# Router logits on four column strips and turned back, ranks by pairwise broadcast comparison, sums zeroed by ScalarE: a two-layer encoder trunk on one core

## The reference

```
logits = t @ router_w + router_b                     # 256 x 1024 by 1024 x 16
probs  = softmax(logits).reshape(N, 4, 4)            # 4 groups of 4 experts
group_score = top_k(probs, 2)[0].sum(-1)
g_sel  = argmax(group_score)
in_group = probs of group g_sel                      # 4 values
w_top, i_top = top_k(in_group, 2); w_top /= w_top.sum()
out[token] = sum over its 2 experts of w * (silu(x @ w_gate[e]) * (x @ w_up[e])) @ w_down[e]
```

## Time and profile before

| | us |
|---|---|
| median of 3 runs | 1472.39 |
| lowest, highest | 1471.46, 1472.82 |
| the profiled execution | 1469.38 |
| its span, first to last instruction | 1467.6 |
| PE busy | 1160.6 (79%) |
| DVE busy | 411.4 (28%) |
| ACT busy | 169.8 (12%) |
| POOL busy | 21.4 (1%) |
| mean granted TensorE clock | 0.876 |

### The profile page before, as it was taken

How to read it: one execution, slowest core, us unless ns; L and a number is a source line. 1 busy time by engine, 2 the same in 40 slices (tenths; PEclk the granted TensorE clock), 3 DMA queues, 4 the chain that set the end, 5 groups by cost and what they waited for, 6 DMA issues and landing times.

```text
span 1467.6 us, 30503 instructions
## 1 busy us (share of the span) xinstructions
PE 1160.6 (79%) x13016; PEld 662.9 (45%) x13016; DVE 411.4 (28%) x1293; ACT 169.8 (12%) x411; POOL 21.4 (1%) x58
## 2 busy tenths in 40 slices
PE   2799978767989779766799868788679987788675
PEld 0684434434545335333374754344345654354332
DVE  0597063211222212121611141642112231121115
ACT  0003110000111001000101130111011110010001
POOL 3100000000000000000000000000000000000000
PEclk7899968888999889888889999769889998899887
DMA  9809859999999999999954301759999699999980
GB/s 373 352 19 422 358 234 408 426 424 426 366 395 413 426 426 423 423 427 421 416 201 167 115 1 58 286 225 426 425 424 393 283 389 424 427 426 422 425 357 29
DMA packets 49282, 494.70 MB, mean 337 GB/s; under 512 B 4231, under 2 KB 4247, under 8 KB 8988
## 3 DMA queue, kind: packets, MB, share of 16 engines
q1 hardware_dynamic: 48176, 490.75, 80.4%
q10 hardware_dynamic: 684, 2.32, 0.4%
q0 software_dynamic: 320, 0.16, 0.1%
HBM read 492.17 MB, written 1.05 MB: 336 GB/s over the span
## 4 chain that ended last, share of the span: by engine, by line
PE 55%; DMA 31%; DVE 8%; ACT 2%; issue 2%; ACTq 0%; DVEq 0%; POOL 0%; POOLq 0%
PE PS L898 24%; DMA ring<-in_w_up_dram 17%; DMA ring<-in_w_gate_dram 13%; PE PS L802 6%; PE PS L820 4%; PE PS L1005 4%; PE PS L926 3%; PE PS L736 3%; PE PS L879 2%; DMA work<-in_conv_ln_b_dram 2%; PE PS L1138 1%; DVE work L1356 1%; PE PS L889 1%; DVE xs L1210 1%; PE PS L786 1%
## 5 line engine op out<-in xcount | busy, mean ns | idle before, releaser
L898 PE MATMUL PS<-ring,work 128*32 128x256 f32 x8064 | 521.0, 415 | 112.1 <-DMA ring<-in_w_gate_dram 53.3
L898 PEld LDWEIGHTS PS<-ring,work 128*32 128x32 f32 x8064 | 278.7, 118 | 344.3 <-issue 104.7
L1374 DVE TENSOR_TENSOR work<-work,PS 128x256 f32<-128x256 f32 x47 | 19.8, 422 | 541.9 <-PE PS L898 541.9
L802 PE MATMUL PS<-ring,work 128*128 128x512 f32 x192 | 83.1, 593 | 0.5 <-ACT work L693 0.5
L898 PE MATMUL PS<-work 128*32 128x256 f32 x960 | 65.7, 420 | 15.4 <-DMA work<-in_w_up_dram 14.6
L736 PE MATMUL PS<-ring,crep 128*32 128x512 f32 x448 | 62.2, 711 | 18.8 <-DVE crep L1420 11.2
L926 PE MATMUL PS<-work 32*128 32x256 f32 x784 | 74.0, 503 | 3.1 <-ACT work L598 1.0
L916 PE MATMUL PS<-ident,work 128*128 128x128 f32 x94 | 23.1, 332 | 64.1 <-DVE work L1360 64.1
L1455 DVE SCALAR_TENSOR_TENSOR work<-work,colv 128x256 f32<-128x256 f32 x150 | 64.2, 487 | 1.2
L820 PE MATMUL PS<-work,ring 128*128 128x256 f32 x256 | 58.2, 391 | 1.9 <-DVE work L1188 1.9
L879 PE MATMUL PS<-hs,work 128*32 128x256 f32 x784 | 55.8, 403 | 3.8 <-DVE work L1347 3.8
(11 more groups left out here) (218 smaller groups left out, 802.5 us busy)
## 6 DMA issues: line engine op xcount, KB each, us to landing
ring<-in_w_gate_dram SPq DMA_DIRECT2D x64, 2048.0 KB, 25.7
ring<-in_w_up_dram SPq DMA_DIRECT2D x54, 2048.0 KB, 26.3
ring<-in_w_down_dram SPq DMA_DIRECT2D x54, 2048.0 KB, 29.0
ring<-in_w_ada_dram SPq DMA_DIRECT2D x24, 2048.0 KB, 17.7
work<-in_w_up_dram SPq DMA_DIRECT2D x10, 2048.0 KB, 26.1
work<-in_w_down_dram SPq DMA_DIRECT2D x10, 2048.0 KB, 27.7
ring<-in_w_pw_dram SPq DMA_DIRECT2D x6, 2048.0 KB, 39.0
ring<-in_w_ada_kv_dram SPq DMA_DIRECT2D x4, 2048.0 KB, 14.8
```

The source lines that it names most:

```text
L802: last = pe.matmul(PS[:, banks + 2 * t + q, :], hT[:, k, t * P:(t + 1) * P], quarter(index + h, kk, KH)[:, q * BANK:(q + 1) * BANK], start ...
L898: last = pe.matmul(dst[SLOTS * s:SLOTS * (s + 1), :], rows[:, cc, SLOTS * q:SLOTS * (q + 1)], quarter(load + h, kk, KH)[:, QUART * s:QUART ...
L1374: dve.tensor_tensor(hh, hh, up_ps, ALU.mult).then_inc(hh_ready, 1)
```

## The change

Four edits:

- Logits: `rw` becomes the stationary operand, two blocks' columns (32) at a time, on four column strips; `hT` streams, 256 columns. Eight matmuls, four into bank `B_GATE`, four into `B_M`; in each strip 16 of the 32 rows are wanted. ACT copies the first bank to SBUF, DVE the second (`parts`). Four matmuls with `parts` as the stationary operand against 16 columns of `lane`, a 0/1 tile, pick the wanted rows, add the strips and turn the result back to tokens by experts, in bank `B_UP`. The first load into `spare` now waits for `logits_parted`.
- Ranks: one "greater" and one "greater or equal" over all pairs at once (8 x 4 x 4 = 128 values, then 2 x 4 x 4 = 32), a mask for the lower index, a maximum, a sum: five instructions in place of ten.
- Zeros: ACT writes banks 0 to 3 behind the exponential, PE's `zero_sums` is gone, PE waits for `sums_zeroed` before the first `sum_x`.
- The owed `half_free` of layer 0 is given by the first matmul of the first `sum_x`.

POOL makes the mask `lower` (a memset and a select) where it made `later` (four memsets).

The diff; declarations of tiles and semaphores are left out:

```diff
             def load(index, source):
                 if index in opens:
-                    sp.wait_ge(logits_done, opens[index] + 1)
+                    sp.wait_ge(logits_parted, 2 * opens[index] + 2)
...
-            for v in range(PER):
-                last = pool.memset(later[:, :, v:v + 1], float(PER - 1 - v))
-            last.then_inc(consts, 1)
+            pool.memset(lower[:, :, :], 1.0).then_inc(consts, 1)
...
+            pool.affine_select(out=lower[:, :, :], in_=lower[:, :, :], compare_op=ALU.is_gt, fill=0.0, base=0,
+                               pattern=[[1, PER], [-1, PER]], channel_multiplier=0).then_inc(consts, 1)
...
             def moe(l):                                                  # ScalarE
+                act.wait_ge(logits_parted, 2 * l + 1)
+                act.activation(parts[:, 0, :], PS[:, B_GATE, 0:SEQ], ACT.Copy).then_inc(parts_kept, 1)
                 act.wait_ge(lmax_ready, l + 1)
                 act.activation(r_ex[:, :, :], r_ex[:, :, :], ACT.Exp).then_inc(lexp_ready, 1)
+                act.wait_ge(hT_copied, 4 * (2, 5)[l])
+                for b in range(4):
+                    act.activation(PS[:, b, :], ones[:, 0:1].to_broadcast([P, BANK]), ACT.Copy,
+                                   scale=0.0).then_inc(sums_zeroed, 1)
...
             def moe(index, l):                                           # TensorE
+                for kk in range(2):
+                    for q in range(4):
+                        last = pe.matmul(PS[32 * q:32 * q + 32, (B_GATE, B_M)[kk], 0:SEQ],
+                                         rw[:, 2 * q:2 * q + 2, :].rearrange("p k e -> p (k e)"), hT[:, 2 * q + kk, :],
+                                         start=True, stop=True, tile_position=(0, 32 * q), skip_group_check=True)
+                    last.then_inc(logits_parted, 1)
+                pe.wait_ge(parts_kept, l + 1)
+                pe.wait_ge(parts_copied, l + 1)
                 for t in range(TT):
-                    for k in range(KD):
-                        last = pe.matmul(PS[:, B_GATE, t * E:(t + 1) * E], hT[:, k, t * P:(t + 1) * P],
-                                         rw[:, k, :], start=(k == 0), stop=(k == KD - 1))
+                    for kk in range(2):
+                        last = pe.matmul(PS[:, B_UP, 2 * E + t * E:2 * E + (t + 1) * E],
+                                         parts[:, kk, t * P:(t + 1) * P], lane[:, kk * E:(kk + 1) * E],
+                                         start=(kk == 0), stop=(kk == 1))
                 last.then_inc(logits_done, 1)
-                def zero_sums():
-
-                    for b in range(4):
-                        behind(pe.matmul(PS[:, b, :], ident[0:1, 1:2].to_broadcast([1, P]), hs[0:1, 0, 0:BANK],
-                                         start=True, stop=False, skip_group_check=True))
-
-                if l > 0:
-                    zero_sums()
...
                 if l == 0:
-                    zero_sums()
                     pe.wait_ge(ada_added, 5)
...                                                                       # sum_x
+                            if t == q == 0:
+                                behind(last)
...
                 pe.wait_ge(routed, l + 1)
+                pe.wait_ge(sums_zeroed, 4 * (l + 1))
                 sum_x(pe.snap(n_pe) + 1)
...
-            def ranks(rank, compared, values, n):
-
-                for d in range(1, n):
-                    link(dve.tensor_tensor(compared[:, :, 0:n - d], values[:, :, 0:n - d], values[:, :, d:n], ALU.is_ge))
-                    link(dve.tensor_tensor(rank[:, :, d:n], rank[:, :, d:n], compared[:, :, 0:n - d], ALU.add))
-                    link(dve.tensor_tensor(rank[:, :, 0:n - d], rank[:, :, 0:n - d], compared[:, :, 0:n - d], ALU.subtract))
+            def ranks(rank, values, rows):
+
+                n = values.shape[-1]
+                mine = values.unsqueeze(3).to_broadcast([P, rows, n, n])
+                others = values.unsqueeze(2).to_broadcast([P, rows, n, n])
+                dve.tensor_tensor(r_gt[:, 0:rows], others, mine, ALU.is_gt)
+                link(dve.tensor_tensor(r_ge[:, 0:rows], others, mine, ALU.is_ge))
+                link(dve.tensor_tensor(r_ge[:, 0:rows], r_ge[:, 0:rows],
+                                       lower[:, :, :].unsqueeze(1).to_broadcast([P, rows, n, n]), ALU.mult))
+                link(dve.tensor_tensor(r_ge[:, 0:rows], r_ge[:, 0:rows], r_gt[:, 0:rows], ALU.max))
+                link(dve.tensor_reduce(rank, r_ge[:, 0:rows], AX.X, ALU.add))
...
             def moe(l):                                                  # VectorE
-                lg = PS[:, B_GATE, 0:TT * E].rearrange("p (t e) -> p t e", t=TT)
+                lg = PS[:, B_UP, 2 * E:2 * E + TT * E].rearrange("p (t e) -> p t e", t=TT)
+                dve.wait_ge(logits_parted, 2 * l + 2)
+                dve.tensor_copy(parts[:, 1, :], PS[:, B_M, 0:SEQ]).then_inc(parts_copied, 1)
                 dve.wait_ge(logits_done, l + 1)
...
-                link(dve.tensor_copy(r_rk[:, :, :], later[:, :, :]))
-                ranks(r_rk, r_c, pg, PER)
+                ranks(r_rk[:, :, :], pg, 2 * GROUPS)
...
-                link(dve.tensor_copy(r_gr[:, :, :], later[:, 0:TT, :]))
-                ranks(r_gr, r_gc, r_gs, GROUPS)
+                ranks(r_gr[:, :, :], r_gs[:, :, :], TT)
```

More of the change, by code:

```diff
@@ L153, in trunk_kernel @@
         plus1 = sb("plus1", [P, 3])
-        later = sb("later", [P, 2 * GROUPS, PER])
+        lower = sb("lower", [P, PER, PER])
         eps = sb("eps", [P, 1])
@@ L161, in trunk_kernel @@
         r_p = sb("r_p", [P, TT, E])
-        r_c = sb("r_c", [P, 2 * GROUPS, PER])
         r_rk = sb("r_rk", [P, 2 * GROUPS, PER])
@@ L165, in trunk_kernel @@
         r_gs = sb("r_gs", [P, TT, GROUPS])
-        r_gc = sb("r_gc", [P, TT, GROUPS])
         r_gr = sb("r_gr", [P, TT, GROUPS])
@@ L200, in trunk_kernel @@
         r_pos = part(TT * E, to="p (t e) -> p t e", t=TT)
+        r_ge = part(2 * GROUPS * PER * PER, to="p (r i j) -> p r i j", i=PER, j=PER)
+        r_gt = part(2 * GROUPS * PER * PER, to="p (r i j) -> p r i j", i=PER, j=PER)
         assert at[0] <= 7168 + KD * SEQ - EXTRA * KH * D
         spare = work[:, 7168 + KD * SEQ - KH * D:7168 + KD * SEQ]
+        parts = work[:, 0:2 * SEQ].rearrange("p (b t) -> p b t", b=2)
         at[0] = 0
@@ L290, in trunk_kernel @@
         ln_sd = sem("ln_sd")
+        sums_zeroed = sem("sums_zeroed")
+        logits_parted = sem("logits_parted")
+        parts_copied = sem("parts_copied")
+        parts_kept = sem("parts_kept")
         logits_done = sem("logits_done")
@@ L370, in stacks @@
             return tile[:, (i % 2) * D:(i % 2 + 1) * D].rearrange("p (g m c) -> p g m c", g=4, c=32)
-        CONSTS = 26
+        CONSTS = 27
         COLROWS = 16 * 5
```

## The result

The changed kernel takes 1460.19 us (median of 6 runs, 1457.19 to 1467.99), the kernel before 1471.41 in the same comparison: a ratio of 0.9927 [0.9899, 0.9954], 11.2 us less. The forecast was 1466.4 with a range from 1462.5 on; the gain is larger than the range allowed. The profiled execution of the changed kernel took 1467.99 us (span 1466.2, mean granted clock 0.882).

The account below looks back on a forecast made before the run. The restart of weight transfers after each router stage was taken as the bound. Layer 0's 2.07 and layer 1's 3.96 us sum to 6.0, taken from a median of 1472.39 (3.0 above the profiled execution): 1466.4 us, range 1462.5 to 1470.2.

Parts of the forecast that it names:

- What bounds the stage: Router stages: the restart of transfers is set in layer 0 by the logits, in layer 1 by the whole router path.
- the third rival: Layer 0 held by PE, not transfers: 6.6 us of `sum_x` count instead of 2.07; sum 10.5, time 1461.9; chance 0.07.
- The logits: Both router stages: new logits take 2.89 us for 4.96 and 5.18, saving 2.07 in layer 0, 2.29 in layer 1.
- The first rival: Low granted clock in the logits: they gain only 0.65 and 0.87 us; sum 3.2, time 1469.2; chance 0.18.
- The ranks: DVE's selection: ten steps of 2.70 us replace 4.17, saving 1.47 in each layer, on the path only in layer 1.
- The zeros: Zeros moved from PE to ACT: 0.2 us saved in layer 1, where they held back the counting.
- The exponential's table: ACT's table load behind its new copy, both layers: hidden by 1.2 us; with a drain, 0.2 us late per layer.
- The owed release: Layer 0, SP's fourth load waits for `sum_x`: release near 225.5, 7 us before transfers run dry at 232.7; no cost.
- the fourth rival: SP's queue, layer 0: `sum_x` after about 232.7 idles transfers, eating the 6.0 us gain at 238.7; chance 0.07.
- A shift of the restart passes to the end: Behind each router stage's restart: an earlier restart shortens the whole time equally, as nothing waits for an absolute time.
- The sum of the parts: Both router stages: layer 0 saves 2.07 us, layer 1 2.29 + 1.47 + 0.2 = 3.96, together 6.0.
- the text's last sentence: If both restarts come early but the end does not, the clock in stretches PE holds is most likely why.

Follow-up runs that it names:

- e4: Kernel before with only the zeros written by ScalarE (ACT) and the owed release in the first gather: 1472.74 us, ratio 0.9998 [0.9985, 1.0011].
- e7: Changed kernel, unaltered, run for a third profile: 1462.06 us, ratio 0.9939 [0.992, 0.9958] to the kernel before; its profiled execution took 1457.30 us.
- e17: Kernel before, unchanged, run for a last profile: its profiled execution took 1475.31 us, with logits of 7.05 us in both layers.

## Why the prediction was right or wrong

- **What bounds the stage.** Right. Layer 0's restart follows the first ada half in every profile, layer 1's the first strip of the first expert. That layer 0 is held by transfers and not by `sum_x` (the third rival) is shown by the loads: `sum_x` comes 12.4 us behind the first issue before and 7.8 after, and the seventh load behind it lands 38.5 us behind it in both. The zeros alone (e4) bring `sum_x` 3 us forward and gain nothing.
- **The logits.** The forecast had 2.07 + 2.29 = 4.36; the means of the table give 2.72 + 1.70 = 4.42. But that is luck in part. The price of the new logits was bounded on both sides, and both bounds were met: 2.78 at the full clock, 4.47 at the half clock (4.31 in the text). Within it the four matmuls take 1.04 us at their best and not 1.35, the copy with its two semaphores 0.64 and not 0.50. The price of the old ones was read from one profile, 4.96 and 5.18, and left without a bound. They take 7.05 at the half clock, in five of ten stages. At a like clock the saving is 2.2 us (full, the old logits in their first part only) or 2.6 (half); between unlike states it runs from 0.5 to 4.3 in a layer.
- **The first rival** put the clock low in the new logits alone: 0.18, and 3.2 us in sum. The low clock came in seven of twelve stages, but the old kernel has it in five of ten, so it does not take the gain away.
- **The ranks.** 2.50 us for the ten steps (1.50 + 1.00) instead of 2.70: two steps of each rank lie partly under each other (0.21 from the first to the second). The saving is 1.63, the forecast had 1.47, and it counts only with the zeros off PE.
- **The zeros.** 0.2 in the sum, in company with the ranks; right in the sum, and the text didn't say that each of the two is worth nothing without the other.
- **The exponential's table.** Hidden. In the third profile of the changed kernel (e7), layer 1, where the logits are fastest, the load runs from 940.92 to 942.20 and the exponential starts at 943.27, behind DVE. By the Trainium skill, ScalarE: Activation LUTs, section What ACT_TABLE_LOAD costs, a drain of about 1.38 us follows the load; by an estimate from it the exponential would have come at 943.58. This run shows no such drain.
- **The owed release.** No hole in the transfers, as priced; issues at 216.26, 221.09 and 225.12, and the fourth rival's 232.7 was never near.
- **The step that failed** is the one from the stage to the end: "A shift of the restart passes to the end", because behind it "everything is either transfers in a row or PE work that starts on a landed load", and the saving of one execution set against the median. The sum of the parts, 6.0, was near the 6.3 that the profiles show. But the stage behind layer 0's restart became 2.3 us shorter itself, which had no term: PE holds a stretch of it, where one strip takes 1.93 us in place of 3.3 to 3.5 in four of six profiles, and the text's last sentence named the clock in such stretches only as what could take the gain away. And the median of before lies above the mean of its profiles (1471.4 against 1470.6) while that of after lies below (1460.2 against 1463.7), where the text let both stand 3.0 above. The range failed on the gain side because the price of the old logits had no bound: with both at 7.05 the text's own sum gives 10.0 us, 1462.4, already outside, and e17 and e7 lie 10.9 apart in their router stages. It was not among the rivals. How much of the measured 11.2 us this makes in the timed runs is not shown; what is left beyond 6.9 stays open.

## What to carry to other kernels

Where a stage is short matmuls behind idle time, take the price of what goes out from several executions and bound it as carefully as what comes in; here one profile had it at 5 us and another at 7. Two edits that lie side by side on different engines can be worth nothing alone and all of their sum together: ask of each what holds the next step once it is gone. And a serial stage on PE can be made shorter by giving PE more to do ahead of it: five unused matmuls in an idle stretch of each router stage took some 10 us off the kernel before, of which its profile shows 3.3 in those stages.

## What the runs showed of the hardware

- The granted clock in the same stretch of the same program differs from one execution to the next: 0.50 over transposes and logits in one, 0.61 and then 0.91 in another. By the Trainium skill, TensorE: Matmul & The Clock Gate, Part 4: PE-mode transpose, the full clock doesn't engage for transposes. Here it rose in a stretch that held only transposes (e7, 204.5 to 209.0 us) and in others it did not, so the trace contradicts it for these float32 transposes in some executions.
- Stages that no edit touches take times in steps: the attention stage 210.1, 213.4, 215.5, 217.0 or 218.7 us over the eleven profiles of the two kernels. One profile of a kernel can lie some 5 us from the middle for that alone.
- ACT wrote 512 columns of PSUM in 0.53 us per bank, 2.13 for four, while PE's four matmuls of one row took 7.19 us at the half clock and 3.69 to 5.12 in other stretches.
